# Three low parts of weight tiles from GpSimd to VectorE, and two reorderings, in the first mixer of a fused two-block model

## The chip, the cores and the metric

One core of a Trainium2 chip runs the whole program. The metric is device time in microseconds (us) of one execution: the median over the runs of the kernel.

## The reference, cut to what matters

The reference is two transformer-like blocks, one after the other, on a sequence of 512 tokens of width 1024. The change lies in the first layer's mixer of the first block, a gated linear recurrence with 6 heads of width 128, beside which runs an attention over a memory of 256 tokens:

```python
def hgrn2_mixer(z, lb, onorm_g):           # q, f, i, g = columns of z
    q = silu(q) * 128**-0.5
    fg = lb + (1 - lb) * sigmoid(f);  k = 1 - fg;  v = i
    # per chunk and head: b = cumsum(log fg)
    #   o = (q e^b) @ state + (sum_k q decay k) @ v
    #   state = state * e^(b_last) + (k e^(b_last - b))^T @ v
    return rms_norm(o, onorm_g) * silu(g)
def memory_attention(qm, mem_n, ...):      # 4 heads of 64 over 256 memory tokens
    p = softmax(q k^T / 8);  o = p v
x = x + concat([y, m]) @ w_out             # then the feed-forward part
```

All matrices are float32.

## The kernel before, in words

Each weight matrix comes in tiles ("slots") of 128 x 2048 values, 1 MB each, numbered through the whole program. SyncE loads slot s into `wraw` (two buffers), once `lo_ready` says that slot s-2 is split. ScalarE copies it into the rounded high part `whi` (L1298, semaphore `hi_ready`), and GpSimd, called POOL in the profile, subtracts: `wlo = wraw - whi` (the helper `lo`, L1182, semaphore `lo_ready`). TensorE then makes three matmuls for each product: high by high, low by high, high by low (`three`, L393). VectorE takes the sums out of PSUM (`emptied`). Every engine runs its own program in the order in which it is written; semaphores order them against each other.

**The levels.** The decay products of the mixer are built by doubling: level k = 0 to 7, each in two halves of three heads (`hf`).
- TensorE (loop over k at about L650 to L675): for each half, the small matmuls of `hk` by `hq` (L661 at k=0, L664 and L665 at k=1 to 6, L667 at k=7), then one half of a weight slot, 24 matmuls of 512 columns (L393). Slots S_Z0B+3 to S_Z0B+6 are used here, two levels each. A half of level k waits until VectorE and POOL are through with the same half of level k-1.
- VectorE (L1992, L1997): for each half a multiplication of `hq` (128x768) and a masked copy of the new scores from PSUM into `hA`; after odd levels `take_z0` (L1890) empties the slot.
- POOL (L1208, L1210): for each half the multiplication of `hk` (128x768), which the next level's matmuls wait for, and a smaller one of `hb`. After levels 1, 3 and 5 it also makes the low part of slot S_Z0B+5, S_Z0B+6 and S_O0 = S_Z0B+7 (`if k in (1, 3, 5)`), each first used two or three levels later or after the levels.

**The states.** After level 7, for heads n = 0 to 5: TensorE transposes the keys (`key_transposes`, L686), a copy takes them to SBUF (`keys_by_token`: even n on ScalarE, L1411, odd n on VectorE, L2005), TensorE multiplies keys by values (`key_values`, L696), and VectorE makes the states of three chunks from it (`states`, L1870 and L2014). `key_values(n)` uses one of two PSUM banks and waits for `states(n-2)`. VectorE's order is written out by hand: copy 1, states 0, copy 3, states 1, copy 5, the two `query_norm` (L2022), states 2, states 3, `gated(0)`, states 4. TensorE's: ..., transposes 4, `head_out(0)`, values 3, transposes 5, values 4, values 5, `mem_scores(0)`.

**The loop over n = 0 to 8** couples the heads' outputs with eight steps of memory attention. TensorE: `head_out(n+1)` (L707, L709), `head_sum(n)` (L718; from n=6 on, `out_part` instead: 12 matmuls of the output projection, L533 to L535), `mem_transposes(n-1)` (L735), `mem_scores(n+1)` (L724, after ScalarE's exponentials of step n), `mem_values(n-1)` (L746). ScalarE: exponentials of step n (L1449), `head_hi(n-1)` (L1427), `head_square(n+1)` (L1423), and the root from `head_sum(n)` (L1460, L1461); at n=5 also the high part of slot S_O0+1. VectorE: maximum (L2058), `head_norm(n-1)` (L2037), reciprocal and scaling of the exponentials (L2065, L2068), `gated(n+1)` (L2031), the copy of the transposed probabilities `ptm` (L2078), `low(n-1)` (L2041).

Of the kernel before, what the change touches and what calls it, by code (L numbers as in the profile page):

```python
# [35 lines left out]
S_Z0B = S_M + 4  # L36
# [61 lines left out]
def build(nc, dr, out):  # L98
# [125 lines left out]
    with ExitStack() as ctx:  # L224
# [160 lines left out]
        def _(pe):  # L385
# [314 lines left out]
            def head_out(h):  # L700
                pe.wait_ge(st_s, h + 1)
                if h >= 2:
                    pe.wait_ge(ho_u, h - 1)
                    pe.wait_ge(ho_sq, h - 1)
                for c in range(4):
                    t = slice(c * P, (c + 1) * P)
                    last = mm(ps[:, 2 + h % 2, t], hv[:, c, h * P:(h + 1) * P], hA[:, h, t], start=True, stop=(c == 0))  # L707
                    if c:
                        last = mm(ps[:, 2 + h % 2, t], hS[:, c - 1, h, :], hq[:, h, t], start=False, stop=True)  # L709
                last.then_inc(ho_mm, 1)  # L710
# [51 lines left out]
            for n in range(9):  # L762
                if n < 5:
                    head_out(n + 1)
                if n < 6:
                    head_sum(n)
                else:
                    if n == 6:
                        pe.wait_ge(ho_u, 6)
                        pe.wait_ge(ho_sq, 6)  # L770
                        pe.wait_ge(lo_ready, S_O0 + 1)
                    out_part(S_O0, 2 * n - 12, 2 * n - 10, Y0_ORDER, y_lo, 0, y0_act)
                if n:
                    mem_transposes(n - 1)
                if n < 7:
                    pe.wait_ge(e_ex, 2 * n + 2)
                    mem_scores(n + 1)
                if n:
                    mem_values(n - 1)
            pe.wait_ge(e_ex, 16)  # L780
# [395 lines left out]
        @block.gpsimd  # L1176
        def _(pool):
            def lo(s, i=None, wd=SLOT):

                n = s + 1 if i is None else 2 * i + (s + 1)  # L1180
                pool.wait_ge(hi_ready, n)
                nc.gpsimd.tensor_tensor(wlo[:, s % 2, 0:wd], wraw[:, s % 2, 0:wd], whi[:, s % 2, 0:wd].bitcast(F32),  # L1182
                                        ALU.subtract).then_inc(lo_ready, 1)

            def lo_many(s0, n, wd=SLOT):
                if n % 2:
                    lo(s0, wd=wd)
                s0 += n % 2
                if n < 2:
                    return  # L1190
                with pool.Fori(0, n // 2) as i:
                    for u in range(2):
                        lo(s0 + u, i, wd)

            nc.gpsimd.memset(cspad[:], 0.0).then_inc(cs_zero, 1)
            lo_many(2, S_M + 2)
            for s in range(S_Z0B, S_Z0B + 5):
                lo(s)

            for k in range(1, 8):  # L1200
                h = 1 << k - 1
                for hf in range(2):
                    n = 2 * k + hf - 2
                    pool.wait_ge(lv_mm, 2 * k + hf + 1)
                    if k > 1:
                        pool.wait_ge(lv_t, n - 1)
                    left, total = pairs(hk, hf, h)[:, :, 0:h], pairs(hb, hf, h)
                    nc.gpsimd.tensor_tensor(left, left, spread(total[:, :, 2 * h - 1:2 * h], h), ALU.mult).then_inc(lv_k, 1)  # L1208
                    pool.wait_ge(lv_k, n + 1)
                    nc.gpsimd.tensor_tensor(total[:, :, 2 * h - 1:2 * h], total[:, :, h - 1:h], total[:, :, 2 * h - 1:2 * h],  # L1210
                                            ALU.mult).then_inc(lv_t, 1)
                if k in (1, 3, 5):
                    lo(S_Z0B + 5 + k // 2)
            lo_many(S_O0 + 1, S_D0 - S_O0 - 1)
            lo_many(S_D0, 16, DSLOT)
            lo_many(S_Z1, 4)
            lo(S_UQ, wd=1152)
            lo(S_UQ + 1, wd=1024)

            def rope(n, x, dst):  # L1220
                pool.wait_ge(m_gain, n + 1)
                if n:
                    pool.wait_ge(m_sq, 5 * n - 2)
                else:
                    pool.wait_ge(rp_a, 2)
                nc.gpsimd.tensor_tensor(dst, x, cosT[:], ALU.mult).then_inc(m_rp, 1)

            def rope_add(n, dst):
                if n:
                    pool.wait_ge(m_ev, taken(n - 1, 7))  # L1230
                else:
                    pool.wait_ge(rot_rd, 1)
                pool.wait_ge(m_rp, 2 * n + 1)
                nc.gpsimd.tensor_tensor(dst, dst, rtmp[:, 1, :], ALU.add).then_inc(m_rp, 1)

            rope(0, z1[:, 7, :], kr0[:])
            rope_add(0, kr0[:])
            for pr in range(3):
                rope(pr + 1, rtmp[:, 0, :], mqr[:, pr, :])
                if pr < 2:  # L1240
                    lo(S_UQ + 2 * pr + 2, wd=1152)
                else:
                    lo(S_O1)
                rope_add(pr + 1, mqr[:, pr, :])
                if pr < 2:
                    lo(S_UQ + 2 * pr + 3, wd=1024)
            lo_many(S_O1 + 1, S_D1 - S_O1 - 1)
            lo_many(S_D1, 16, DSLOT)
            lo_many(S_QKV, 8)

            def bias(p):
                cb, hp = p // 4, p % 4
                off = (0, -8, -8, -16)[cb] + 16
                for e in range(2):
                    u = 2 * p + e
                    if u >= 4:
                        pool.wait_ge(w_mx, u - 3)
                    nc.gpsimd.tensor_tensor(wbm[:, u % 4, :].rearrange("p (r c) -> p r c", c=32), wbias[:, :, 2 * hp + e, off:off + 32],
                                            cc("winmask", 32 * cb, 32).unsqueeze(1).to_broadcast([P, 8, 32]),
                                            ALU.add).then_inc(bm_ready, 1)  # L1260

            pool.wait_ge(b_in, 128)
            bias(0)
            bias(1)
            lo(S_GC)
            for n in range(16):
                if n < 14:
                    bias(n + 2)
                if n % 4 == 3:
                    lo(S_GC + 1 + n // 4)  # L1270
            lo_many(S_GC + 5, NS - S_GC - 5)
# [523 lines left out]
        def _(dve):  # L1795
# [181 lines left out]
            for k in range(8):  # L1977
                for hf in range(2):
                    dve.wait_ge(lv_mm, 2 * k + hf + 1)
                    if k == 0:  # L1980
                        for h in range(3 * hf, 3 * hf + 3):
                            last = STT(out=hA[:, h, :].rearrange("p (c t) -> p c t", t=P), in0=ps[:, h, :].rearrange("p (c t) -> p c t", t=P),
                                       scalar=SC, in1=cc("ident").unsqueeze(1).to_broadcast([P, 4, P]), op0=ALU.mult, op1=ALU.mult)
                        last.then_inc(lv_cp, 1)
                        q = hq[:, 3 * hf:3 * hf + 3, :]
                        STT(out=q, in0=q, scalar=SC, in1=hb[:, 3 * hf:3 * hf + 3, :], op0=ALU.mult, op1=ALU.mult).then_inc(lv_q, 1)
                        continue
                    h = 1 << k - 1
                    if k > 1:
                        dve.wait_ge(lv_t, 2 * k + hf - 3)  # L1990
                    right = pairs(hq, hf, h)[:, :, h:2 * h]
                    TT(right, right, spread(pairs(hb, hf, h)[:, :, h - 1:h], h), ALU.mult).then_inc(lv_q, 1)  # L1992
                    n, l = 64 // h, 7 - k
                    msk = cc("lvl", 64 * l, 64).bitcast(U32).rearrange("p (g t) -> p g t", t=h)
                    src = ps[:, 3 * hf:3 * hf + 3, :].rearrange("p a t -> p (a t)").rearrange("p (c g t) -> p c g t", c=12, t=2 * h)[:, :, :, h:2 * h]
                    dst = hA[:, 3 * hf:3 * hf + 3, :].rearrange("p a t -> p (a t)").rearrange("p (c g t) -> p c g t", c=12, t=2 * h)[:, :, :, h:2 * h]
                    V.copy_predicated(dst, msk.unsqueeze(1).to_broadcast([P, 12, n, h]), src).then_inc(lv_cp, 1)  # L1997
                if k % 2:
                    take_z0(S_Z0B + 3 + k // 2)

            dve.wait_ge(lv_t, 14)
            link(V.tensor_copy(chunk_decay.rearrange("p (h c) -> p h c", c=4), hb[:].rearrange("p h (c t) -> p h c t", t=P)[:, :, :, P - 1]))
# [41 lines left out]
            states(0)  # L2044
            keys_by_token(3)
            states(1)
            keys_by_token(5)
            query_norm(0)
            query_norm(1)
            states(2)  # L2050
            states(3)
            gated(0)
            states(4)
# [613 lines left out]
```

## Time and profile before

| | us |
|---|---|
| median of three runs | 1869.66 (1869.33, 1872.64, 1869.66) |
| the profiled execution | 1868.17 |
| its span, first to last instruction | 1866.3 |
| TensorE busy in the span | 1811.0 (97%) |
| VectorE, ScalarE, POOL busy | 932.8, 729.7, 714.6 |
| mean granted clock of TensorE | 0.993 |

The profile lists for each engine its instructions with start and length, and the idle time in front of one with what released it. The granted clock is 1.00 at TensorE's full 2.4 GHz and 0.50 at 1.2 GHz. The levels lie from 171.5 to 251 us of the span, the states from 252 to 265, and the loop over n from 265 to 311.

### The profile page before, as it was taken

What the parts mean: (1) busy time and instruction counts of PE and PEld (TensorE: products, weight loads), DVE (VectorE), ACT (ScalarE), POOL (GpSimd) and SP (SyncE); (2) the same over time, 40 slices, a digit from 0 to 9 for tenths busy, and PEclk for the clock granted to TensorE, in tenths of its full rate; (3) what the DMA queues carried; (4) which work ended last, traced back from release to release, by engine and by line L of the source; (5) the groups of instructions that cost most, each with busy time, mean ns of one, the idle gap of its engine ahead of it and who ended that gap; (6) DMA issues with size and microseconds to landing.
All of it is one profiled execution on the core that took longest, in us unless ns stands there. A gap on an engine that the chain in (4) does not pass through costs nothing.

```text
span 1866.3 us, 24525 instructions
## 1 busy us (share of the span) xinstructions
PE 1811.0 (97%) x9589; PEld 1473.8 (79%) x9589; DVE 932.8 (50%) x1287; ACT 729.7 (39%) x960; POOL 714.6 (38%) x224
## 2 busy tenths in 40 slices
PE   7989988999999999999999999999999999999998
PEld 5789766888888887666888888888887788888886
DVE  4365775465554116576446555334427734413564
ACT  4142134455554224454455555322314542221423
POOL 1253821444343444321244334344244333344332
PEclk9999999999999999999999999999999999999999
DMA  7632101222322223111122322333421122332211
GB/s 285 254 113 91 47 23 40 97 90 96 107 90 78 93 100 98 48 48 44 55 104 90 105 98 76 102 100 123 86 75 61 46 69 89 112 105 95 86 68 68
DMA packets 28185, 170.33 MB, mean 91 GB/s; under 512 B 3024, under 2 KB 5328, under 8 KB 11728
## 3 DMA queue, kind: packets, MB, share of 16 engines
q1 hardware_dynamic: 24720, 151.20, 23.5%
q10 hardware_dynamic: 3392, 18.09, 2.9%
q8 instruction: 54, 0.88, 0.2%
q14 instruction: 19, 0.16, 0.0%
HBM read 167.18 MB, written 2.10 MB: 91 GB/s over the span
## 4 chain that ended last, share of the span: by engine, by line
PE 69%; issue 17%; POOL 7%; DVE 5%; ACT 2%; DMA 0%; POOLq 0%; ACTq 0%; DVEq 0%
PE ps L393 41%; PE ps L808 12%; POOL wlo L1182 5%; POOL hk L1208 1%; PE ps L1073 1%; PE ps L1056 1%; PE ps L533 1%; PE ps L1085 1%; PE ps L1083 1%; PE ps L1084 1%; PE ps L535 1%; PE ps L534 1%; PE ps L899 1%; PE ps L413 1%; PE ps L415 1%
## 5 line engine op out<-in xcount | busy, mean ns | idle before, releaser
L1182 POOL TENSOR_TENSOR wlo<-wraw,whi 128x2048 fp32r<-128x2048 f32 (+3 forms) x151 | 641.9, 4251 | 1035.3 <-ACT whi L1298 1017.4
L393 PE MATMUL ps<-hh,whi 128*128 128x512 f32 x1344 | 527.8, 393 | 1.4 <-POOL wlo L1182 0.8
L393 PE MATMUL ps<-hh,wlo 128*128 128x512 f32 x1344 | 523.2, 389 | 0.0
L393 PE MATMUL ps<-hl,whi 128*128 128x512 f32 x1344 | 523.1, 389 | 0.0
L1298 ACT ACTIVATE whi<-wraw 128x2048 fp32r<-128x2048 f32 (+3 forms) x149 | 265.2, 1780 | 371.4 <-PE ps L393 299.1
L393 PEld LDWEIGHTS ps<-hh,whi 128*128 128x128 f32 x1344 | 252.3, 188 | 57.2 <-issue 3.2
L393 PEld LDWEIGHTS ps<-hl,whi 128*128 128x128 f32 x1344 | 252.4, 188 | 53.0 <-issue 1.2
L393 PEld LDWEIGHTS ps<-hh,wlo 128*128 128x128 f32 x1344 | 252.3, 188 | 52.9
L2142 DVE SCALAR_TENSOR_TENSOR scr<-ps,vec,scr 128x510 f32<-128x510 f32 (+1 forms) x176 | 120.1, 744 | 93.1 <-ACT scr L1502 93.1
L808 PE MATMUL ps<-gh,whi 128*128 128x512 f32 x352 | 137.7, 391 | 1.3 <-DVE gl L2157 1.3
L808 PE MATMUL ps<-gh,wlo 128*128 128x512 f32 x352 | 137.0, 389 | 0.0
L808 PE MATMUL ps<-gl,whi 128*128 128x512 f32 x352 | 137.0, 389 | 0.0
L2169 DVE TENSOR_TENSOR xT<-xT,ps 128x512 f32<-128x512 f32 x16 | 11.0, 687 | 174.1 <-PE ps L808 174.1
L808 PEld LDWEIGHTS ps<-gh,whi 128*128 128x128 f32 x352 | 66.1, 188 | 16.5 <-issue 2.1
L808 PEld LDWEIGHTS ps<-gh,wlo 128*128 128x128 f32 x352 | 66.1, 188 | 13.8
L808 PEld LDWEIGHTS ps<-gl,whi 128*128 128x128 f32 x352 | 66.1, 188 | 13.4
L2154 DVE TENSOR_TENSOR scr<-scr 128x512 f32<-128x512 f32 x44 | 67.2, 1527 | 4.6
L2138 DVE TENSOR_TENSOR ps<-ps,rstdn 128x512 f32<-128x512 f32 x44 | 30.8, 699 | 76.3 <-PE ps L393 56.2
L1502 ACT ACTIVATE scr<-ps,vec 128x512 f32<-128x512 f32 x88 | 62.8, 764 | 0.0
L1312 ACT ACTIVATE hh<-xT,vec 128x512 fp32r<-128x512 f32 x32 | 22.9, 719 | 97.4 <-DVE xT L2169 55.5
L1507 ACT ACTIVATE gh<-scr 128x512 f32 x44 | 27.8, 632 | 77.5 <-DVE scr L2154 77.5
L1298 ACT ACT_TABLE_LOAD x22 | 28.2, 1283 | 58.5 <-PE ps L393 58.5
(460 smaller groups left out, 2807.2 us busy)
## 6 DMA issues: line engine op xcount, KB each, us to landing
wraw<-in_w SPq DMA_DIRECT2D x63, 1024.0 KB, 4.9
wraw<-in_w0b SPq DMA_DIRECT2D x26, 1024.0 KB, 4.8
wraw<-in_w1o SPq DMA_DIRECT2D x26, 1024.0 KB, 4.9
wraw<-in_wd SPq DMA_DIRECT2D x32, 704.0 KB, 4.0
ada<-in_wada ACTq DMA_DIRECT2D x12, 1024.0 KB, 7.9
xtok<-in_x SPq DMA_DIRECT2D x4, 512.0 KB, 8.7
out<-ytok SPq DMA_DIRECT2D x4, 512.0 KB, 4.0
wraw<-in_w SPq DMA_DIRECT2D x3, 576.0 KB, 3.9
```

What stands on the lines that cost most here:

```text
L393: last = mm(o, l, r, start=(k == 0 and n == 0), stop=(k == K - 1 and n == 2))
L413: mm(o, w_(0, k), x(0, k), start=(j == 0), stop=False)
L415: last = mm(o, w_(1, k), x(0, k), start=False, stop=(j == 7))
L808: last = mm(ps[:, 4 + n, :], (whi, wlo)[a][:, par, k * P:(k + 1) * P], (gh, gl)[b][:, 11 * hf + k, :], start=(hf == 0 and k == 0 and m == ...
L1182: nc.gpsimd.tensor_tensor(wlo[:, s % 2, 0:wd], wraw[:, s % 2, 0:wd], whi[:, s % 2, 0:wd].bitcast(F32), ALU.subtract).then_inc(lo_ready, 1)
L1298: A(whi[:, s % 2, 0:wd], wraw[:, s % 2, 0:wd], ACT.Copy).then_inc(hi_ready, 1)
L1312: A(hh[:, k, :], xT[:, k, :], ACT.Copy, scale=vv(g, k)).then_inc(nx_hi, 1)
L1502: A(scr[:, 2 * u + ab, :], ps[:, 2 * par + ab, :], ACT.Identity, bias=vec[:, bass.ds(2 * i + col, 1)], scale=vec[:, bass.ds(2 * i + wc, 1) ...
L1507: A(gh[:].rearrange("p c t -> p (c t)")[:, bass.ds((2 * i + u) * T, T)], scr[:, 2 * u, :], ACT.Copy).then_inc(f_hi, 1)
L2138: TT(pa, pa, rstdn[:], ALU.mult).then_inc(f_sc, 1)
L2142: STT(out=dst[:, d:T], in0=src[:, 0:T - d], scalar=vec[:, bass.ds(2 * i + col, 1)], in1=dst[:, d:T], op0=ALU.mult, op1=ALU.add).then_inc(s ...
L2154: TT(a, a, b, ALU.mult).then_inc(f_g, 1)
```

## The change

Three things. First, POOL no longer makes the low parts of the three slots after levels 1, 3 and 5; VectorE makes them after levels 2, 4 and 6, behind its two halves, once `hi_ready` says that the high part is there. Second, in VectorE's order `states(2)` stands ahead of the two `query_norm`, and `keys_by_token(5)` behind them. Third, in TensorE's loop over n, `mem_transposes(n-1)` and the wait for the exponentials with `mem_scores(n+1)` stand ahead of `head_sum(n)` (or of `out_part` from n=6 on). No instruction is added or dropped otherwise.

```diff
@@ -762,6 +762,11 @@
             for n in range(9):
                 if n < 5:
                     head_out(n + 1)
+                if n:
+                    mem_transposes(n - 1)
+                if n < 7:
+                    pe.wait_ge(e_ex, 2 * n + 2)
+                    mem_scores(n + 1)
                 if n < 6:
                     head_sum(n)
                 else:
@@ -770,11 +775,6 @@
                         pe.wait_ge(ho_sq, 6)
                         pe.wait_ge(lo_ready, S_O0 + 1)
                     out_part(S_O0, 2 * n - 12, 2 * n - 10, Y0_ORDER, y_lo, 0, y0_act)
-                if n:
-                    mem_transposes(n - 1)
-                if n < 7:
-                    pe.wait_ge(e_ex, 2 * n + 2)
-                    mem_scores(n + 1)
                 if n:
                     mem_values(n - 1)
             pe.wait_ge(e_ex, 16)
@@ -1209,8 +1209,6 @@
                     pool.wait_ge(lv_k, n + 1)
                     nc.gpsimd.tensor_tensor(total[:, :, 2 * h - 1:2 * h], total[:, :, h - 1:h], total[:, :, 2 * h - 1:2 * h],
                                             ALU.mult).then_inc(lv_t, 1)
-                if k in (1, 3, 5):
-                    lo(S_Z0B + 5 + k // 2)
             lo_many(S_O0 + 1, S_D0 - S_O0 - 1)
             lo_many(S_D0, 16, DSLOT)
             lo_many(S_Z1, 4)
@@ -1997,6 +1995,10 @@
                     V.copy_predicated(dst, msk.unsqueeze(1).to_broadcast([P, 12, n, h]), src).then_inc(lv_cp, 1)
                 if k % 2:
                     take_z0(S_Z0B + 3 + k // 2)
+                if k in (2, 4, 6):
+                    s = S_Z0B + 4 + k // 2
+                    dve.wait_ge(hi_ready, s + 1)
+                    TT(wlo[:, s % 2, :], wraw[:, s % 2, :], whi[:, s % 2, :].bitcast(F32), ALU.subtract).then_inc(lo_ready, 1)
 
             dve.wait_ge(lv_t, 14)
             link(V.tensor_copy(chunk_decay.rearrange("p (h c) -> p h c", c=4), hb[:].rearrange("p h (c t) -> p h c t", t=P)[:, :, :, P - 1]))
@@ -2044,10 +2046,10 @@
             states(0)
             keys_by_token(3)
             states(1)
-            keys_by_token(5)
+            states(2)
             query_norm(0)
             query_norm(1)
-            states(2)
+            keys_by_token(5)
             states(3)
             gated(0)
             states(4)
```

## Rows read from the trace of the kernel before

**Rows 1.** The page: TensorE's busy time, and the chain that ended last by engine.
```profile
PE 1811.0 (97%) x9589; PEld 1473.8 (79%) x9589; DVE 932.8 (50%) x1287; ACT 729.7 (39%) x960; POOL 714.6 (38%) x224
...
PE 69%; issue 17%; POOL 7%; DVE 5%; ACT 2%; DMA 0%; POOLq 0%; ACTq 0%; DVEq 0%
```

**Rows 2.** Waits of TensorE, 168 to 256 us: total, times, longest.
```profile
PE ps L664 <- POOL hk L1208: 4.5, 4, 1.5
...
PE ps L667 <- POOL hk L1208: 1.0, 2, 0.8
```

**Rows 3.** Busy time by stretch: length, PE, PEld, DVE, ACT, POOL, clock, DMA share, GB/s.
```profile
184.20:192.90 8.70, 8.70 (x123) 7.40 (x124) 5.68 (x4) 0.00 (x0) 6.92 (x3) 1.00 0.01 2
```

**Rows 4.** Timeline of POOL: start, length, instruction, idle before and releaser.
```profile
215.42 5.00 POOL L1182 TENSOR_TENSOR wlo<-wraw,whi 128x2048 fp32r<-128x2048 f32 x1 [1.81 <-ACT whi L1298]
```

**Rows 5.** Groups by line, 168 to 256 us: busy in total, mean ns, idle before.
```profile
L1992 DVE TENSOR_TENSOR hq<-hq,hb 128x768 f32<-128x768 f32 x14 | 27.8, 1984 | 10.2 <-PE ps L665 7.8 <-PE ps L667 2.2
L1208 POOL TENSOR_TENSOR hk<-hk,hb 128x768 f32<-128x768 f32 x14 | 27.7, 1978 | 9.6 <-PE ps L665 9.6
...
L1182 POOL TENSOR_TENSOR wlo<-wraw,whi 128x2048 fp32r<-128x2048 f32 x4 | 19.6, 4908 | 12.6 <-ACT whi L1298 12.6
...
L1997 DVE COPY_PREDICATED hA<-con,ps 128x768 f32<-128x768 uint32 x14 | 17.8, 1272 | 0.0
```

**Rows 6.** VectorE's instructions that write `wlo`: ns min/median/max, starts.
```profile
L1849 DVE TENSOR_TENSOR wlo<-wraw,whi x2: 2281/2287/2293, 11.1 to 26.6; 128x2048 fp32r<-128x2048 f32 x2
```

**Rows 7.** Timeline of VectorE beside POOL's low part at 215.42.
```profile
216.77 4.47 DVE L1992 TENSOR_TENSOR hq<-hq,hb 128x768 f32<-128x768 f32 x1
```

**Rows 8.** Timeline of TensorE, VectorE and ScalarE in the states, 257 to 267 us.
```profile
259.58 0.49 PE L686 MATMUL ps<-con,hk 128*128 128x128 f32 x3
263.09 2.29 PE L696 MATMUL ps<-hv,hk 128*128 128x128 f32 x12 [3.02 <-DVE hS L2014]
...
266.47 1.22 PE L707 MATMUL ps<-hA,hv 128*128 128x128 f32 x4
...
260.11 0.56 DVE L2005 COPY hk<-ps 128x384 f32<-128x384 f32 x1 [2.79 <-PE ps L686]
...
261.89 0.28 DVE L1870 TENSOR_SCALAR hS<-ps 128x128 f32<-128x128 f32 x1
...
257.96 0.58 ACT L1417 ACTIVATE ps<-ps 128x512 f32<-128x512 f32 x1
```

**Rows 9.** Busy time by stretch, with the granted clock, around the two drops.
```profile
260.90:264.40 3.50, 1.25 (x9) 1.12 (x10) 3.36 (x9) 0.00 (x0) 0.00 (x0) 1.00 0.00 0
264.40:267.80 3.40, 3.40 (x16) 2.52 (x15) 2.19 (x7) 0.49 (x3) 0.00 (x0) 0.50 0.00 0
...
295.10:298.50 3.40, 3.40 (x10) 2.53 (x9) 2.80 (x2) 1.02 (x4) 3.40 (x1) 0.50 0.01 2
```

**Rows 10.** Timeline of ScalarE: root of n=0, exponentials of n=1.
```profile
269.81 0.66 ACT L1460 ACTIVATE ps<-ps,con 128x512 f32<-128x512 f32 x1 [0.27 <-PE ps L718]
...
271.18 0.47 ACT L1449 ACTIVATE prm<-ps,small 128x256 f32<-128x256 f32 x1
```

**Rows 11.** The chain that ended last, same step of n=3 and n=4.
```profile
279.83 0.61 DVE small L2058
...
284.48 0.61 DVE small L2058
```

**Rows 12.** End of the loop: PE at n=5, ScalarE, VectorE at n=6.
```profile
289.27 1.10 PE L718 MATMUL ps<-sqx,con 128*128 128x512 f32 x2
...
290.82 0.70 PE L724 MATMUL ps<-km,qm 64*128 64x256 f32 x4
...
294.62 0.47 ACT L1449 ACTIVATE prm<-ps,small 128x256 f32<-128x256 f32 x1
...
295.86 3.91 DVE L2068 TENSOR_SCALAR prm<-prm,small 128x256 f32<-128x256 f32 x2
```

**Rows 13.** Waits of TensorE, 251 to 312 us: total, times, longest.
```profile
PE ps L746 <- DVE ptm L2078: 5.7, 8, 1.9
```

## The prediction

> **What bounds the kernel now.** I read the page first. TensorE is busy 97% of the span, and the chain that ended last is mostly TensorE and its issue; POOL holds 7% of it [rows 1]. So outside the first mixer a microsecond saved is carried to the end unless a wait absorbs it, and with TensorE this full there is little to absorb it. Next the waits of TensorE in the levels: it stood 4.5 us at levels 2 to 6 and 1.0 us at level 7, each time for POOL's multiplication of `hk` [rows 2]. Nothing else stopped it there. Level 1 ran without a wait: TensorE was busy for all 8.70 us of its stretch, so about 8.7 us is what a level costs TensorE alone [rows 3]. POOL falls behind because of its third job: the low part at 215.42 held it for 5.00 us between two levels [rows 4], and it made three of these inside the levels.
>
> In the states I read the timelines side by side. TensorE ended the transposes of head 5 at 260.07 and then stood 3.02 us, up to 263.09, for a state [rows 8]. It was states(2). VectorE could have made it long before: it had stood idle for 2.79 us in front of copy 5, which stands ahead of it in the program; then came the two query norms; and states(2) began only at 261.89 [rows 8]. In the loop over n TensorE waits 5.7 us in eight places for the copy of the transposed probabilities [rows 13].
>
> **Edit 1: three low parts from POOL to VectorE.** On POOL three instructions go, of 4.9 us mean [rows 5]. With them goes its lag. What is left for POOL is 14 multiplications of `hk`, 27.7 us [rows 5], and the `hb` ones, about half of that, over seven levels of 8.7 us = 60.9 us: no queue builds up. Gain: the whole 5.5 us of [rows 2]. Bounds: nothing (POOL held up as before) and 6.1 us, if each of the six waits also hid 0.1 us of restart.
>
> On VectorE three instructions come in, of 2.29 us, from the two it makes of the same shape at the start of the program [rows 6]. Its own work in the levels is 27.8 + 17.8 us [rows 5], to which the 2 x 4 take-outs add about 5 us. Of the 27.8 us a part is waiting: the multiplication at 216.77 took 4.47 us beside POOL's low part, until that ended at 220.42, where it takes about 1 us alone [rows 4, 7]. A VectorE multiplication with both inputs in SBUF and a POOL instruction do not run at the same time; one waits for the other. Three such waits of about 3 us each go away with POOL's low parts (-9), and 3 x 2.29 = 6.9 come in. VectorE then has 27.8 + 17.8 + 5 - 9 + 6.9 = about 48.5 us in 60.9. Within an even level it is tight: two multiplications of 1 us, two masked copies of 1.27 us mean and the low part of 2.29 make 6.8, plus up to 2 us for each of three waits for POOL. It may start the next level 2 or 3 us late, but what TensorE needs from that level is wanted only after 24 large matmuls (8.7 us later), and odd levels hold no low part. So I cost it at nothing; the cover is about 3 us per low part, and past it each us is TensorE's.
>
> The wait that is added, for `hi_ready`, has the next level's multiplications queued behind it. ScalarE made the high parts right as levels 2, 4 and 6 began, and VectorE reaches the wait a level's work later: no cost. The loads of SyncE wait for `lo_ready`; the low parts come 2 to 5 us after where they were, but a slot is used two levels (17 us) later, and a load of 4.9 us fits: nothing.
>
> Here a rule of the notes speaks against the edit. In the rows the two engines exclude each other, as said. The Trainium skill, Perfetto Trace Analysis, section Optimizing Scalar/DVE Operations, says that GpSimd and VectorE share an SBUF read port, "so offloading operations between those two might not help". By it, edit 1 would be worth little, since VectorE's low part still shuts POOL out. The sum goes by the rows: the exclusion now lasts 2.29 us in place of 4.9.
>
> **Edit 2: states(2) ahead.** VectorE's idle 2.79 us in front of copy 5 begin at 257.32 [rows 8], behind states(1), and TensorE's values 2, which states(2) needs, stand ahead of `head_out(0)`, long before. So states(2), 1.05 us, ends by about 258.5, in idle time. The query norms need ScalarE's roots, done at 258.54 [rows 8]; two at 0.65 us end at about 259.9, before the transposes of head 5 do (260.07). Copy 5 starts as before, at 260.11. `key_values(4)` no longer waits: 260.1 instead of 263.09, a gain of 3.0 us. What is late next is `key_values(5)`: it needs copy 5 and states(3), which follow each other on VectorE, 0.5 + 1.05 us after 260.11, so it starts at 261.7 where it started at 264.06. That is 2.4 us; TensorE waits about 0.9 us there. On top comes the clock. The stretch from 264.4 ran at 0.50 (1.2 GHz), after a stretch in which TensorE had been busy only 1.25 of 3.5 us [rows 9]; `key_values(5)`, the first scores and `head_out(1)` fell in it, and `head_out`'s first four matmuls took 1.22 us [rows 8]. Without the long wait I expect full clock, and `head_out(1)` to begin at about 263.1 instead of 266.47 [rows 8]: 3.3 us in all. Bounds: 2.4 (the clock falls all the same) and 4.5 (`head_out(1)` also runs its own 2.3 us in 1.7, and all of it counts).
>
> **Edit 3: transposes and scores ahead of the sum.** At n=0: the scores of step 1 (0.6 us) and their wait for the exponentials now stand ahead of `head_sum(0)`. ScalarE's root came straight after that sum, at 269.81, and with its second half (0.58) ran up to 1.27 us later; the exponentials of n=1 followed at 271.18 [rows 10]. There was no slack, so the ring starts 0.7 us later: a loss of 0.7. At n=1 to 4 the same step comes every 4.65 us [rows 11], and the ring is exponentials, `head_hi`, square (ScalarE), `gated`, copy of `ptm`, low part, maximum (VectorE): TensorE is not in it. Its wait of 0.3 us for `ptm` merely moves. Cost and gain nothing; the root, 0.9 us later, then ends just ahead of the next exponentials, which is all the cover. At n=5 the sum, which began at 289.27, is behind scores which must wait until 290.82 [rows 12]; 0.6 us for them and 0.9 for the sum end it at 292.3, where ScalarE started the root at about 291.6: the root is 0.7 us later, and with it the high part and the exponentials of n=6, at 294.62 before [rows 12]. At n=6 the scores of step 7 wait for these ahead of 12 large matmuls: they end at about 294.62 + 0.7 + 0.95 = 296.3, and TensorE, through with the values and transposes at about 294.7, stands 1.6 us. On the other side, in 295.1 to 298.5 TensorE ran at 0.50 before [rows 9], and then waited for `ptm` all the same, because VectorE's scaling took 3.91 us beside POOL [rows 12]; and at n=7 and 8 the transposes now come ahead of 12 large matmuls, which hide the copy, so two waits of 0.8 us of the 5.7 [rows 13] go. By that the last values end 0.8 us earlier. Net of edit 3: +0.7 - 0.8 = -0.1. Bounds: +2.5 (the clock falls after the two new waits, in the large matmuls) and -1.5.
>
> **Sum.** -5.5 - 3.3 - 0.1 = -8.9 us. Against the profiled execution, 1868.17, that gives 1859.3. The median of the runs shown is 1.5 us above that execution, so 1860.8.
>
> **The rivals.**
> - *The order eats the states' gain.* Edit 3's waits at n=5 and 6 lower the clock for another stretch of 3.4 us, in which large matmuls run at half speed (1.7 us lost), and n=0 costs 0.7: net -8.9 + 2.5 = -6.4, 1863.3. For it: two waits of 1.1 and 1.6 us close together. Against: such a stretch is there already [rows 9].
> - *The port.* VectorE's low part shuts POOL out just when it wants to start a level, and half of POOL's lag stays: -2.7 in place of -5.5, 1863.6. This is what the skill's sentence, cited above, comes to here. Against: 2.29 is less than half of 4.9, and POOL has some 20 us to spare over the levels.
> - *Both of these*, or edit 1 worth nothing: -3.3 to -3.6, about 1866.2.
> - *Slower: VectorE becomes the bound of the levels.* The low part stands ahead of the next level's two multiplications. If each takes its 2.29 us, the 3.5 us that the multiplication lost beside POOL [rows 7], and two further turns of POOL (2 us each, [rows 5]), it is about 9.8 us; less its own 2.29 and the cover of 3, TensorE waits 4.5 us three times: +13.5 in place of -5.5 in the levels, with the other edits: 1868.17 + 13.5 - 3.4 + 1.5 = 1879.8. It makes the kernel slower by 0.2% from about 7.7 us per low part on. Against: the sum of 48.5 us in 60.9.
>
> That an edit does nothing at all is out for edit 2 (the wait and its cause are both in the rows) and is priced for edit 1.
>
> **How the numbers follow.** Forecast 60%; order 16%; port 13%; both 7%; slower 4%. About 0.2% (3.7 us) is what a measurement of this kernel can tell from no change. Forecast, order and port are all faster by more than that (89%); I take 2 off, as the runs shown already spread over 3.3 us. Of the 7% most is within it. The range from 1857.8 (upper bound of edit 2, 0.6 more of edit 1, and a run as low as the profiled one) to 1864.9 takes in order and port with 1.3 us over them.
>
> **What would show it.** In the changed profile: no or under 0.5 us of waits of TensorE for POOL in the levels, level 7 starting about 5.5 us earlier; three low parts on VectorE of 2.3 to 4 us; `key_values(4)` without a wait and one of about 0.9 us ahead of `key_values(5)`; no 0.50 stretch near the first scores; a period of 4.65 us in the loop; waits of about 1.6 us at n=6. TensorE waiting for `hq` would make edit 1 wrong; a period above 4.65 us would make edit 3 wrong.

## The result, and the profile after

The changed kernel took 1857.39 us (median of four runs), the one before 1869.49: ratio 0.994, 95% interval 0.9923 to 0.9957. That is 12.1 us, where 8.9 were forecast, and 0.4 us below the lower end of the range, 1857.8. Part of the distance is the sample: in a later series with five more runs it took 1857.96 against 1868.31 (ratio 0.9944, 0.9931 to 0.9958, so 7.8 to 12.9 us less), and over all 46 runs of the kernel before that are on record the median is 1868.03. By the medians the change is worth 10 to 11 us.

The profiled execution spans 1854.6 us, where before it was 1866.3. The page, busy times and chain by engine [rows 1]:

```profile
PE 1807.7 (97%) x9589; PEld 1471.0 (79%) x9589; DVE 931.0 (50%) x1290; ACT 729.7 (39%) x960; POOL 708.0 (38%) x221
...
PE 72%; issue 16%; DVE 4%; POOL 4%; ACT 2%; DMA 0%; POOLq 0%; ACTq 0%; DVEq 0%
```

POOL fell from 7% of the chain to 4%; three instructions went from it to VectorE, whose busy time did not grow (931.0, before 932.8): what it got in work it lost in waiting for POOL, which is counted as busy. The waits of TensorE from 168 to 256 us [rows 2]:

```profile
PE ps L661 <- DVE hv L1883: 1.8, 1, 1.8
PE ps L696 <- DVE hS L2016: 1.0, 1, 1.0
PE ps L696 <- ACT hk L1409: 0.7, 2, 0.5
```

No line with POOL is left. The three low parts on VectorE, with its next multiplication and POOL's instruction beside the first of them (timeline, start and length) [rows 4, 6, 7]:

```profile
198.14 3.40 DVE L2001 TENSOR_TENSOR wlo<-wraw,whi 128x2048 fp32r<-128x2048 f32 x1
201.46 1.67 DVE L1990 TENSOR_TENSOR hq<-hq,hb 128x768 f32<-128x768 f32 x1
...
213.87 3.36 DVE L2001 TENSOR_TENSOR wlo<-wraw,whi 128x2048 fp32r<-128x2048 f32 x1
...
231.00 2.94 DVE L2001 TENSOR_TENSOR wlo<-wraw,whi 128x2048 fp32r<-128x2048 f32 x1
...
197.20 2.19 POOL L1208 TENSOR_TENSOR hk<-hk,hb 128x768 f32<-128x768 f32 x1
199.47 2.85 POOL L1210 TENSOR_TENSOR hb<-hb 128x384 f32<-128x384 f32 x1
```

Each is 2.9 to 3.4 us long, not 2.29: it first waits until POOL's `hk` ends (197.20 + 2.19 = 199.39), and then holds POOL's `hb` until 201.5, which takes 2.85 us for work of 0.9. The states, TensorE and VectorE [rows 8]:

```profile
251.33 0.49 PE L686 MATMUL ps<-con,hk 128*128 128x128 f32 x3
251.66 0.83 PE L696 MATMUL ps<-hv,hk 128*128 128x128 f32 x6
253.53 0.91 PE L696 MATMUL ps<-hv,hk 128*128 128x128 f32 x6 [1.04 <-DVE hS L2016]
...
254.99 0.71 PE L707 MATMUL ps<-hA,hv 128*128 128x128 f32 x4
...
251.86 0.56 DVE L2007 COPY hk<-ps 128x384 f32<-128x384 f32 x1 [0.51 <-PE ps L686]
```

`key_values(4)` follows the transposes at once; the new wait stands in front of `key_values(5)`. In the loop the waits have moved (TensorE, 244 to 305 us) [rows 13]:

```profile
PE ps L724 <- ACT prm L1447: 3.3, 3, 2.0
PE ps L746 <- DVE ptm L2080: 1.5, 2, 0.9
```

and at n=0, 5 and 6 they stand where the scores now wait or delay the root (ScalarE, then TensorE) [rows 10, 12]:

```profile
258.71 0.66 ACT L1458 ACTIVATE ps<-ps,con 128x512 f32<-128x512 f32 x1 [1.25 <-PE ps L718]
...
259.89 0.47 ACT L1447 ACTIVATE prm<-ps,small 128x256 f32<-128x256 f32 x1
...
279.54 0.70 PE L724 MATMUL ps<-km,qm 64*128 64x256 f32 x4 [1.00 <-ACT prm L1447]
...
285.39 0.70 PE L724 MATMUL ps<-km,qm 64*128 64x256 f32 x4 [1.96 <-ACT prm L1447]
```

To compare kernels I cut the mixer at seven groups of instructions that all of them have, by their starts in the timelines (in brackets those of the kernel before): VectorE's last take-outs of `hv` (169.75), its first multiplication of level 1 (185.85), the first key transposes (252.43), the first memory scores (265.31), ScalarE's exponentials of n=1 (271.18) and of n=6 (294.62), and the last memory values (310.12). The differences are, in us:

| | level 0 | levels 1 to 7 | states | to n=1 | n=1 to 6 | n=6 to 8 | run median |
|---|---|---|---|---|---|---|---|
| before | 16.10 | 66.58 | 12.88 | 5.87 | 23.44 | 15.50 | 1868.03 |
| changed | 14.46 | 60.25 | 10.18 | 5.53 | 24.43 | 14.10 | 1857.96 |
| e1: edit 1 | 16.08 | 60.24 | 12.92 | 5.84 | 23.48 | 15.46 | 1862.95 |
| e2: edit 2 | 16.09 | 66.50 | 10.19 | 4.72 | 23.45 | 15.47 | 1864.56 |
| e3: edit 3 | 14.45 | 66.52 | 12.47 | 5.53 | 24.44 | 14.00 | 1867.04 |
| e4: edits 1, 2 | 14.46 | 60.25 | 10.18 | 4.73 | 23.45 | 15.47 | 1856.06 |
| e5: low part twice | 16.09 | 62.06 | 10.18 | 5.53 | 24.44 | 15.31 | 1861.20 (one) |
| e6: four times | 16.08 | 78.91 | 10.18 | 5.54 | 24.42 | 15.47 | 1879.33 (one) |
| e7: late part of edit 3 | 16.08 | 60.25 | 10.18 | 4.73 | 23.46 | 13.67 | 1856.30 |
| e8: POOL later | 16.11 | 61.71 | 13.49 | 4.82 | 23.44 | 15.48 | 1864.21 |
| e9: level 0 filled | 12.40 | 60.25 | 10.18 | 4.73 | 23.44 | 13.66 | 1855.07 |
| e10: all steps | 12.39 | 60.25 | 9.39 | 4.73 | 22.86 | 12.98 | 1851.83 |

(Before: all 46 runs; changed: all nine; the last column spans several series of runs, so kernels of different series compare by their ratios below.) One of e8's ten runs took 4665 us, for which nothing on record gives a reason; its median counts it, its ratio does not. The columns repeat within 0.1 us wherever the code and the clock are the same, and that is what makes parts of 1 us readable here, although single runs of the kernel before differ by up to 7.5 us. Where the clock differs they don't: e5 and e6 have the loop of the changed kernel and take 15.31 and 15.47 us from n=6 to 8, not 14.10. For the change: 1.6 at level 0, 6.3 in the levels, 2.7 + 0.3 in the states and up to n=1, -1.0 and +1.4 in the loop, 11.4 of the 11.7 us between the spans. The first is not put down to the change: the code up to there is the same in every kernel but e9 and e10, and no edit decides between the two values (with edit 3 14.45 in e3 and 16.09 in e5, with edits 1 and 2 14.46 in e4 and 16.08 in e7).

### The profile page after: what moved, and what is told of

It is laid out like the page before. It is cut to its first block, busy times and chain, and to the rows that moved or that the text cites. A ratio compares the mean times of both kernels' runs of the same rounds, so it can differ in the third digit from the quotient of the medians.

```text
span 1854.6 us, 24525 instructions
## 1 busy us (share of the span) xinstructions
PE 1807.7 (97%) x9589; PEld 1471.0 (79%) x9589; DVE 931.0 (50%) x1290; ACT 729.7 (39%) x960; POOL 708.0 (38%) x221
## 4 chain that ended last, share of the span: by engine, by line
PE 72%; issue 16%; DVE 4%; POOL 4%; ACT 2%; DMA 0%; POOLq 0%; ACTq 0%; DVEq 0%
PE ps L393 43%; PE ps L808 12%; POOL wlo L1182 4%; PE ps L664 1%; PE ps L1073 1%; PE ps L1056 1%; PE ps L533 1%; PE ps L534 1%; PE ps L535 1%; PE ps L1085 1%; PE ps L1083 1%; PE ps L1084 1%; PE ps L899 1%; PE ps L413 1%; PE ps L415 1%
## 5 line engine op out<-in xcount | busy, mean ns | idle before, releaser
L1182 POOL TENSOR_TENSOR wlo<-wraw,whi 128x2048 fp32r<-128x2048 f32 (+3 forms) x148 | 626.8, 4236 | 1025.7 <-ACT whi L1296 1007.7
```

## The experiments

**e1, e2, e3, e4: the three edits apart.** Each is the kernel before with one of the three hunks of the diff (e4 with the first two):

```diff
 e1: -  if k in (1, 3, 5): lo(S_Z0B + 5 + k // 2)            # POOL
     +  if k in (2, 4, 6): ... TT(wlo, wraw, whi, subtract)  # VectorE
 e2: -  keys_by_token(5); query_norm(0); query_norm(1); states(2)
     +  states(2); query_norm(0); query_norm(1); keys_by_token(5)
 e3:    mem_transposes and mem_scores ahead of head_sum / out_part
```

> Edit 1 alone. Theory (the sum of the prediction, mended by the trace of the changed kernel, where level 7 ended 6.3 us earlier than its start at level 1 accounts for): 5.5 to 6.3 us less than before, all of it between level 1 and the end of level 7, with no wait of TensorE for POOL there; the wait of 3.0 us for states(2) stays, and a granted clock of 0.50 somewhere just behind it. Rival (the port): half of the waits stay, about 2.7 us less. Rival (edits need each other): under 4 us less in time.

Measured: 1862.95, ratio 0.9967 (0.9953 to 0.9981), so 3.5 to 8.8 us less. The levels take 60.24 in place of 66.58: 6.3 us, no wait for POOL, and the wait of 3.0 for states(2) is untouched (waits of TensorE, 168 to 315 us):

```profile
PE ps L746 <- DVE ptm L2080: 5.7, 8, 1.9
PE ps L696 <- DVE hS L2016: 3.0, 1, 3.0
PE ps L661 <- DVE hv L1883: 1.8, 1, 1.8
```

The waits are not the whole of the 6.3 us. TensorE's busy time over the levels, before and in the changed kernel, whose levels are those of e1 (length, PE, PEld, DVE, ACT, POOL, clock, DMA share, GB/s):

```profile
185.85:252.43 66.58, 61.12 (x749) 50.73 (x744) 48.99 (x37) 8.58 (x6) 55.95 (x31) 1.00 0.14 49
```
```profile
183.93:244.18 60.25, 60.25 (x749) 50.40 (x744) 47.59 (x40) 8.58 (x6) 49.30 (x28) 1.00 0.16 54
```

It stood 66.58 - 61.12 = 5.5 us before and not at all now, and the same 749 matmuls were busy for 0.9 us less.

> Edit 2 alone. Theory: 3.0 to 3.4 us less between the end of level 7 and the start of head_out(1), of which 2.4 by key_values(5) and the rest by the clock, because the stretch at 0.50 behind the wait is gone; waits for POOL in the levels stay at 5.5 us. Rival: the clock falls all the same, 2.4 us less. In the time of whole runs 1.5 to 4, since an execution with or without a half-clock stretch elsewhere differs by 1.7.

Measured: 1864.56, ratio 0.9984 (0.9975 to 0.9994). States and the stretch to n=1 take 14.91 in place of 18.75: 3.8 us, of which the clock is a part (the stretch behind, 257.4 to 270, ran at 1.00). How large a part depends on the execution that it is compared with. In e3, which has the old order of the states and the same wait, the clock did not fall behind it (timeline of TensorE, then the stretch behind the wait, at 1.00):

```profile
261.07 1.88 PE L696 MATMUL ps<-hv,hk 128*128 128x128 f32 x12 [3.02 <-DVE hS L2014]
```
```profile
260.80:264.20 3.40, 3.07 (x22) 2.49 (x23) 3.09 (x9) 0.00 (x0) 0.00 (x0) 1.00 0.02 5
```

States and the stretch to n=1 take 18.00 us in e3 and 15.71 in the changed kernel, which differs there by edit 2 alone: 2.3 us.

> Edit 3 alone. Theory: +0.2 to +0.7 at n=0, nothing at n=1 to 4 (period 4.65 us), +1.0 at n=6 and -1.4 at n=7 and 8: a net of -0.5 to +0.5 us from head_out(1) to the out projection, same time as before within 0.2%. Rival (the order is what the forecast undervalued, 12.1 us measured against 8.9): 2 to 3 us less.

Measured: 1867.04, ratio 0.9997 (0.9987 to 1.0006): no difference. By the columns +1.0 from n=1 to 6 and -1.5 from n=6 to 8. What it does at n=0 is read between e4 and the changed kernel, where the clock is 1.00 in both: 5.53 against 4.73, +0.8. What it does from n=6 on hangs on the clock behind its two new waits. In the changed kernel (both profiles) and in e3 one stretch of 3.4 us at 0.50 followed them; in e5 and e6, with the same loop, it was 6.8 us. The two halves of it in e5:

```profile
288.60:292.00 3.40, 2.81 (x8) 1.87 (x9) 2.80 (x2) 1.02 (x4) 3.40 (x1) 0.50 0.00 0
292.00:295.40 3.40, 3.40 (x9) 2.43 (x8) 3.04 (x5) 0.32 (x1) 0.84 (x1) 0.52 0.41 104
```

That took the gain of 1.4 us almost whole. Where the scores keep their old place the stretch is there in three of nine profiles (before, e1, e8), and the column is 15.5 us with it and without (e2, e4).

> Edits 1 and 2 without edit 3. Theory: the two add, 9 to 9.5 us less than before, so within 1 us of the changed kernel beside equal clock stretches. Rival (edit 3 is worth 2 to 3 us): this kernel 2 to 3 us slower than the changed one, about 1860.

Measured: 1856.06, ratio 0.9939 (0.9922 to 0.9955), by that 11.4 us less, more than the 6.2 and 3.0 of e1 and e2 together. The columns add exactly (60.25, 10.18, 4.73); 1.6 of the 2.2 us that are over lie in level 0, where e1's and e2's profiled executions had a stretch at half clock and e4's did not. Edit 3 brings nothing on top: net +0.8 + 1.0 - 1.4 = +0.4 us in the columns of the changed kernel, +1.6 and +1.8 in those of e5 and e6.

**e5 and e6: how much VectorE can bear.** The changed kernel with the low part made twice and four times, with a wait between:

```diff
+                    link(TT(wlo[...], wraw[...], whi[...], ALU.subtract))   # once (e5), three times (e6)
                     TT(wlo[...], wraw[...], whi[...], ALU.subtract).then_inc(lo_ready, 1)
```

> The changed kernel with each of VectorE's three low parts made twice, one behind the other (the same values are written twice). It measures the cover. Theory (the price of the edit is hidden, with some 3 us to spare per low part): from level 1 to level 7 at most 1 us longer than the changed kernel's 51.7 us, though VectorE does 3 x 2.3 us more. Rival (VectorE is the bound of the levels): each further 2.3 us is seen in full, 6.9 us longer.

> The changed kernel with each low part made four times (6.9 us more per low part). Theory: the cover of about 3 us is used up, so TensorE waits for VectorE's hq or masked copy, or for POOL held up by it, some 3 to 4.5 us per low part, 9 to 13 us in all between level 1 and the end of level 7, and the kernel is about as slow as the one before or slower. Rival (VectorE is the bound already): 3 x 6.9 = 20.7 us longer. If nothing is seen, the cover is far larger than was reckoned.

Measured: the levels take 62.06 and 78.91, so 1.8 and 18.7 us more. In e6 (timeline of VectorE, then the waits of TensorE from 170 to 275 us):

```profile
201.04 3.37 DVE L2001 TENSOR_TENSOR wlo<-wraw,whi 128x2048 fp32r<-128x2048 f32 x1
204.45 2.90 DVE L2002 TENSOR_TENSOR wlo<-wraw,whi 128x2048 fp32r<-128x2048 f32 x1
207.38 3.79 DVE L2003 TENSOR_TENSOR wlo<-wraw,whi 128x2048 fp32r<-128x2048 f32 x1
211.20 2.85 DVE L2004 TENSOR_TENSOR wlo<-wraw,whi 128x2048 fp32r<-128x2048 f32 x1
213.98 2.56 DVE L1990 TENSOR_TENSOR hq<-hq,hb 128x768 f32<-128x768 f32 x1
```
```profile
PE ps L664 <- DVE hq L1990: 9.6, 2, 6.5
PE ps L632 <- DVE hA L1995: 4.9, 1, 4.9
```

While VectorE made its second low part there, POOL finished one instruction and started the next (its timeline), and so on through the group:

```profile
205.15 3.88 POOL L1208 TENSOR_TENSOR hk<-hk,hb 128x768 f32<-128x768 f32 x1
```

So the three added low parts of this group cost 9.5 us (204.45 to 213.98), not 6.9; those of the other two, with less of POOL's work between them, cost 8.4 and 8.0 (227.90 to 236.32, 249.24 to 257.28), 26.0 us in all. How much of it TensorE saw, by its busy time over the levels:

```profile
186.80:265.71 78.91, 64.17 (x748) 52.70 (x743) 74.67 (x49) 8.70 (x6) 60.71 (x28) 0.94 0.12 41
```

It stood 14.7 us, so 11.3 were hidden, 3.8 us per low part. The other 3.9 of the 18.7 us are busy time: in the levels of e6 the clock was at 0.50 for some 10 us (214.5 to 221.5 and from 262.5 on), in those of the changed kernel never. In e5 the added low parts cost 2.8 + 2.2 + 2.2 = 7.2 us, and 1.8 are seen, all of it behind the first: TensorE waits once, 1.6 us for `hA`. So 5.4 are hidden, 1.0 at the first low part and 2.2, all that was added, at each of the others. The "cover of about 3 us per low part" was near the mean, but it is not the same at each, and what I expected of e6 (9 to 13) was too little, since I had reckoned a low part at 2.3 and no change of the clock.

**e7: only the part of edit 3 that helps.** Edits 1 and 2, with the transposes ahead of `out_part` at n=7 and 8 only:

```diff
-                if n:
+                if n >= 7:
                     mem_transposes(n - 1)
                 if n < 6: head_sum(n)   # or out_part
+                if n and n < 7: mem_transposes(n - 1)
+                if n < 7: ... mem_scores(n + 1)
```

> Edits 1 and 2, and of edit 3 only the part that the traces show to help: the transposes ahead of the 12 large matmuls at n=7 and 8; the old order for n up to 6. Theory: from head_out(1) to the out projection the +0.8 at n=0 and +1.0 at n=6 of the full edit are gone and of its -1.4 at n=7 and 8 about -1.5 stay: 1.5 us less than edits 1 and 2 alone and 2 us less than the changed kernel, about 1855. Rival (the gain at n=7 and 8 comes from the scores of step 7 being early): no gain over edits 1 and 2 alone, 1856.

Measured: 1856.30, ratio 0.9928 (0.9912 to 0.9945); the loop's three columns sum to 41.86, against 43.65 in e4 and 44.06 in the changed kernel, 1.8 and 2.2 us less as expected. In time the gain does not stand out. The same kernel was run once more (e12) beside the changed one (e11):

> The changed kernel once more, on the same chip as the two above, for their comparison and for the spread by clock. Theory: 10.5 us less than before on average (levels 6.3, states 3.2 and the clock behind the wait, edit 3 a loss of 0.4), ratio 0.994; single executions differ by 1.6 us with the clock at level 0. If edit 3 alone explained the distance to the forecast, this one would be faster than the next.

> Edits 1 and 2 with the late part of edit 3 only, once more, beside the changed kernel. Theory: the trace's segments say 2.2 us less than the changed kernel from the first scores to the last values, so a median 1 to 3 us lower. Rival (the clock makes up for it): the same median.

Measured: 1857.96 and 1857.58, ratios 0.9944 (0.9931 to 0.9958) and 0.9940 (0.9927 to 0.9954). The expected 1 to 3 us between the two medians were not found. Their profiled executions differ by 1.6 us at level 0 by the clock (14.49 and 16.10), against the 2.2 of the loop, which five runs don't average out. The loop's gain is shown by its columns, not by the runs.

**e8: place or engine?** The kernel before, POOL's low parts after levels 2, 4 and 6:

```diff
-                if k in (1, 3, 5):
-                    lo(S_Z0B + 5 + k // 2)
+                if k in (2, 4, 6):
+                    lo(S_Z0B + 4 + k // 2)
```

> The kernel before with the low parts still on POOL, but after levels 2, 4 and 6 instead of 1, 3 and 5. It tells apart which part of edit 1 counts, the engine or the place. Theory (POOL's load counts): TensorE still waits for POOL's hk at levels 3 to 6, 3 to 5.5 us; since behind the low part after level 6 the slack is large, up to 1.5 us may be gained; 0 to 2 us less than before. Rival (the place counts): the waits go and 5.5 us are gained, with no work moved to VectorE.

Measured: 1864.21, ratio 0.9977 (0.9966 to 0.9987); the levels take 61.71, which is 4.9 of the 6.3 us. TensorE waits for POOL once (168 to 256 us), though POOL does all its work (its timeline):

```profile
PE ps L664 <- POOL hk L1208: 1.2, 1, 1.2
```
```profile
203.43 4.58 POOL L1182 TENSOR_TENSOR wlo<-wraw,whi 128x2048 fp32r<-128x2048 f32 x1
207.96 2.54 POOL L1208 TENSOR_TENSOR hk<-hk,hb 128x768 f32<-128x768 f32 x1
...
220.56 4.56 POOL L1182 TENSOR_TENSOR wlo<-wraw,whi 128x2048 fp32r<-128x2048 f32 x1
225.08 2.29 POOL L1208 TENSOR_TENSOR hk<-hk,hb 128x768 f32<-128x768 f32 x1
...
231.59 2.30 POOL L1208 TENSOR_TENSOR hk<-hk,hb 128x768 f32<-128x768 f32 x1 [1.20 <-PE ps L665]
```

So the place counts for most of it, and my theory (3 to 5.5 us of waits) fell. In the kernel before, TensorE's waits stood in levels 3, 5 and 7 only: each needs the `hk` of the level ahead of it, and POOL had made a low part before that `hk` (timeline of TensorE before; two such waits in each of these levels):

```profile
203.00 0.24 PE L664 MATMUL ps<-hq,hk 128*64 128x64 f32 x1 [1.51 <-POOL hk L1208]
...
222.88 0.24 PE L664 MATMUL ps<-hq,hk 128*64 128x64 f32 x1 [0.87 <-POOL hk L1208]
...
241.79 1.58 PE L667 MATMUL ps<-hq,hk 128*64 128x64 f32 x24 [0.78 <-POOL hk L1208]
```

After an odd level POOL first had to wait for the high part, which comes only as the next level begins, 1.81 us at 215.42 [rows 4], and then made 5 us of low part ahead of the `hk` multiplications that were wanted. After an even level the high part is there and POOL works through without a stop; by 231.59 it is idle again.

**e9 and e10: a version that beats both.** e9 is e7 with nine large matmuls of level 0 (K = 0 to 2 of the first weight half) ahead of the wait for `hv`:

```diff
+            pe.wait_ge(lo_ready, S_Z0B + 4)
             ...                            # part: `three` cut at K, its matmuls from k0 to k1
+            part(ps[:, 6, :], wv((S_Z0B + 3) % 2, 256), 0, 3)
             pe.wait_ge(emptied, S_Z0B + 3)
             for k in range(8):
                 ...
-                last = three(ps[:, 6 + b, :], wv(s % 2, 256, off=b * P), hv_(), 8)
+                last = part(ps[:, 6 + b, :], wv(s % 2, 256, off=b * P), 3 if k == 0 else 0, 8)
```

> Edits 1 and 2 with the late part of edit 3, and 9 of the 24 large matmuls of level 0 put ahead of its small ones, where TensorE stands 1.8 us for VectorE in every kernel so far. It tests the clock at level 0: the small matmuls of level 0 ran at 0.50 in some executions (levels begin 16.1 us behind VectorE's last take-out of hv) and at 1.00 in others (14.45). Theory (that wait is what lowers the clock there, and by its place against the chip's own time only in some executions): the stretch from that take-out to level 1 is about 14.2 - 1.8 + 0.2, some 12.7 us, in every execution, so 1.8 us less always and 3.4 less where the clock fell before, and no 0.50 at level 0. Rival (the clock falls whatever TensorE does there): 0.50 again in this or the next stretch, 1.8 us less.

Measured: 1855.07, ratio 0.9925 (0.9911 to 0.9939); its five runs (at most 1855.43) lie below all of e11 and e12 (at least 1855.9). Level 0 takes 12.40 us, and three stretches by window show no stop and the full clock (length, PE, PEld, DVE, ACT, POOL, clock, DMA share, GB/s):

```profile
168.00:171.40 3.40, 3.40 (x27) 3.23 (x27) 0.73 (x2) 0.73 (x1) 0.00 (x0) 1.00 0.59 248
171.40:174.80 3.40, 3.40 (x27) 3.17 (x26) 0.93 (x3) 1.19 (x1) 2.14 (x1) 1.00 0.00 0
174.80:178.20 3.40, 3.40 (x32) 3.36 (x31) 2.70 (x4) 0.00 (x0) 2.38 (x1) 1.00 0.06 10
```

e10 adds two steps:

```diff
 ScalarE, loop over n:
-                if n == 5:
+                if n == 6:
                     conv_upto(S_O0 + 1)
 ScalarE, behind head_square(0):
+            act.wait_ge(st_tr, 6)
+            A(hkT[:, 5, 0:3, :], ps[:, 1, 0:3 * P]..., ACT.Copy).then_inc(st_td, 1)
 VectorE:
-            keys_by_token(5)
             states(3)
```

> The kernel above, with two further steps read off the traces: the high part of slot S_O0+1 on ScalarE behind the exponentials of n=6 instead of ahead of them (with it POOL's low part comes later and no longer stops VectorE's scaling for 3.3 us), and copy 5 of the keys on ScalarE behind head_square(0), with states(3) not waiting for it. Theory: 0.9 us less before key_values(5), and 1 to 3 us less at n=6; about 3 less than the kernel above, near 1850. Rival: the ring at n=5 to 8 is bound by the copies of ptm in VectorE's order and only the 0.9 is seen.

Measured: 1851.83, ratio 0.9913 (0.9899 to 0.9926), 16 us under the kernel before. The states take 0.8 us less, the loop 1.3 less (22.86 + 12.98 against 23.44 + 13.66). VectorE's scaling of n=6 takes 0.62 us in place of 3.91 [rows 12]; that of n=7 now meets POOL's low part, for 1.71, so of the 1 to 3 us only the lower end came:

```profile
280.85 0.62 DVE L2083 TENSOR_SCALAR prm<-prm,small 128x256 f32<-128x256 f32 x2
...
286.28 1.71 DVE L2083 TENSOR_SCALAR prm<-prm,small 128x256 f32<-128x256 f32 x2
```

## Why the prediction was right, and where it was off

**The direction and most of the path were right.** The mechanism is the forecast one in each edit: no wait for POOL in the levels, states(2) in VectorE's idle time, the next wait in front of `key_values(5)`, 1.04 us (0.9 forecast), a period of the loop that did not change.

**Edit 1: forecast 5.5, measured 6.3** (e1, e4 and the changed kernel alike), just over the upper bound of 6.1. The waits were 5.5 and are gone; the rest is busy time, 61.12 to 60.25 us for the same matmuls, or 0.15 for each of the six waits, where at most 0.1 was reckoned. That it is the restart behind each stop is argued, not shown. The cost on VectorE was nothing, as forecast, with a cover of about 3 us per low part in the mean, but only about 1 at the first (e5, e6); the low part itself I had at 2.29, and it is 2.9 to 3.4.

The reason given was wrong in one step: "POOL falls behind because of its third job ... With them goes its lag". POOL can do all three jobs in the time of the levels; e8 does them there and keeps 4.9 of the 6.3 us. The bound of "nothing (POOL held up as before)" and the sum of POOL's work over all seven levels didn't ask where within a level a low part stands. Had I set the start of the low part, 215.42, against the start of level 4, I would have seen that it was in the worst place. What the engine adds to the place is 1.5 us (61.71 to 60.25).

**Edit 2: forecast 3.3, measured 3.8 alone** (e2), 2.7 of it up to the scores. Counted from the transposes of head 5, `key_values(4)` comes 3.2 us earlier (forecast 3.0), `key_values(5)` 2.3 (2.4), behind a wait of 1.04 (0.9), and `head_out(1)` 3.2 (3.3). The clock gave 1.1 us between the scores and n=1 (5.87 to 4.72, e2), a little more than I had taken. But this term holds only against an execution in which the clock fell behind the old wait. In e3 it did not, and against it edit 2 is worth 2.3 us, about the lower bound of 2.4. I took one profiled execution for the rule.

**Edit 3: forecast a gain of 0.1, measured a loss of 0.4** beside edits 1 and 2. At n=0 a loss of 0.8 (0.7 forecast); n=1 to 4 nothing; at n=5 and 6 a loss of 1.0, and a gain of 1.4 behind it, net 0.4 where I had 0.8. The two new waits, 1.00 and 1.96 us, are those forecast (1.1, 1.6), and a stretch of lower clock followed them in the changed kernel, as it did before the change. In e5 and e6 it was twice as long, and there the loss is 1.6 and 1.8 us.

**The rest is mostly clock ahead of the edits.** For the last take-out of `hv` TensorE waits 1.8 us in every kernel but e9 and e10. Level 0 then took 16.1 us in some executions and 14.46 in others. In the profiled executions of before and after it fell differently (the same stretch; before, then after):

```profile
172.20:175.60 3.40, 3.40 (x19) 3.40 (x18) 0.00 (x0) 0.00 (x0) 3.40 (x1) 0.50 0.00 0
```
```profile
172.20:175.60 3.40, 3.40 (x33) 3.40 (x32) 1.29 (x3) 0.00 (x0) 3.40 (x1) 1.00 0.00 0
```

That is 1.6 of the 11.7 us between the two profiles. Of the 12.1 us between the first medians, 8.9 was forecast, 0.8 is what edit 1 brought beyond its forecast, and edits 2 and 3 together differ by 0.2 or less (in part luck, as both hang on where the clock falls); the remaining 2.4 are 1.6 of clock at level 0, as far as the profiled executions stand for the others, and the spread of the runs, as the 10.35 us of the later series show. My range started from the median of three runs plus bounds of the edits, and had no term for the clock of stretches that the change doesn't touch. Its lower end is also added up wrongly: 1860.8 less 1.2, 0.6 and 1.5 is 1857.5, not 1857.8. And the rival of the order counts the 0.7 of n=0 a second time, as it is in the forecast already.

**The rivals.** The port: by the sentence of the Trainium skill cited in the prediction (Perfetto Trace Analysis, section Optimizing Scalar/DVE Operations), moving work between these two engines "might not help". The exclusion it rests on is in the trace of the changed kernel (3.40 us for a low part of 2.29, 2.85 for an `hb` of 0.9), but no time was lost by it, as both engines had idle time for it: e1's levels are 6.3 us shorter, not 2.7. The order: edit 3 costs 0.4 us in the profiles of the changed kernel, not the bound of +2.5. Its mechanism, a further stretch of lower clock behind the two waits, is real all the same: e5 and e6 show it, at 1.6 and 1.8 us. Why it came there and not in the changed kernel is open. VectorE as the bound: comes at twice the low part, where e5 shows 1.8 us, and is plain at four times.

## What to carry to other kernels

Ask of a side job on an in-order engine not only how much time the engine has over the whole stage, but which wanted instruction stands right behind it: here most of the gain was to be had by moving the same instruction one level later on the same engine. A wait of TensorE of 1.8 to 3 us cost up to 1.6 us more here when the clock fell behind it (level 0, 16.10 against 14.46), so such a wait is worth filling with matmuls of the next step even if few are at hand (nine in e9). And where runs of one kernel differ by more than the edit is worth, cut the trace at instructions that both kernels have, compare the pieces, and read the granted clock of each: a piece in which it differs says nothing of the edit until a second execution is seen.

## What the runs showed of the hardware that was not expected

The granted clock falls behind the same wait in one profiled execution and not in another: 16.1 or 14.46 us for level 0, nothing between, with the same code and the same wait of 1.8 us; with the wait filled it was 12.40 and 12.39 in the two kernels profiled. The same holds for the wait of 3.02 us in the states: 0.50 behind it before, in e1 and in e8, 1.00 in e3. Of the kernels profiled twice each showed the same value at level 0 both times (changed: 14.46 and 14.49; e7 and e12: 16.08 and 16.10), so what decides it is open.

Also, VectorE's instructions with two SBUF inputs and POOL's take turns as long as both have work: of four low parts in a row on VectorE, which could have followed each other, each of e6's first group let a POOL instruction in ahead of it (2.85 to 3.79 us in place of 2.29).
